# Shift and scale sums of a modulation: from TensorE during the expert gather to GpSimd and ScalarE ahead of it

## The reference, cut to what matters

```
mod_all = silu(c) @ ada_w + ada_b            # c: 1024, ada_w: 1024 x 6144
sh_m, sc_m, gt_m, sh_f, sc_f, gt_f = split(mod_all, 6)
h = rms_norm(x, norm_g[0]) * (1 + sc_m) + sh_m
x = x + gt_m * rms_norm(stick_breaking_mixer(h), norm_g[1])
h = rms_norm(x, norm_g[2]) * (1 + sc_f) + sh_f
x = x + gt_f * rms_norm(swiglu_ffn(h), norm_g[3])
```

## Time and profile before

| | |
|---|---|
| median of 3 runs | 2371.11 us (2367.22 to 2376.46) |
| the profiled execution's own time | 2365.49 us |
| its span | 2363.7 us |
| mean granted TensorE clock | 0.83 |
| PE, DVE, ACT, POOL busy | 76%, 55%, 37%, 38% of the span |
| moved by DMA | 687.78 MB, 536.90 MB of it by the gather's queue |

### The profile page before, as it was taken

The page is one execution under the profiler, slowest core; times in us unless marked ns, Lnnn a source line. Parts: engine busy times, 40 slices in busy tenths (PEclk is TensorE's granted clock), DMA queues, the critical chain, the costliest instruction groups (busy, mean ns, idle before and its releaser), DMA issues. The chain is left out here.

```text
span 2363.7 us, 25240 instructions
## 1 busy us (share of the span) xinstructions
PE 1796.4 (76%) x8848; PEld 1117.7 (47%) x8848; DVE 1291.7 (55%) x2801; ACT 868.9 (37%) x2355; POOL 904.2 (38%) x699
## 2 busy tenths in 40 slices
PE   8898899868777787564443468885377897999998
PEld 6775676445435255110000014331055676888786
DVE  4633668877787665656767676566403623333201
ACT  3122344333444343233643353333225734222212
POOL 1300334374663444344555544445400122444343
PEclk9999888777788889786555679986579998999999
DMA  6111999999999999999999999999953011122121
GB/s 246 54 63 49 403 410 392 418 377 411 411 401 418 418 418 417 417 404 406 419 420 420 419 405 419 418 397 419 420 178 110 1 72 71 72 107 107 72 107 54
DMA packets 108494, 687.78 MB, mean 291 GB/s; under 512 B 12240, under 2 KB 13264, under 8 KB 40144
## 3 DMA queue, kind: packets, MB, share of 16 engines
q0 software_dynamic: 73728, 536.90, 55.3%
q1 hardware_dynamic: 34640, 149.27, 16.9%
HBM read 681.40 MB, written 2.10 MB: 289 GB/s over the span
## 5 line engine op out<-in xcount | busy, mean ns | idle before, releaser
L747 PE MATMUL ps<-arena 128*32 128x512 f32 (+5 forms) x4376 | 872.7, 587 | 377.0 <-ACT arena L1452 337.3
L1696 POOL DMA_INDIRECT arena<-in_experts,arena_u x512 | 608.6, 1189 | 770.9 <-PE ps L747 678.2
L2001 DVE CUSTOM_DVE_ANT_0 arena<-arena 128x1024 f32<-128x1024 f32 x512 | 653.2, 1281 | 384.3 <-DMA arena<-in_experts,arena_u 367.5
L747 PEld LDWEIGHTS ps<-arena 128*128 128x128 f32 (+2 forms) x4376 | 443.2, 167 | 735.5 <-ACT arena L1452 496.6
L1448 ACT ACTIVATE sel<-sel 128x1 f32<-128x1 f32 x512 | 102.8, 201 | 705.4 <-DVE sel L2001 697.7
L1717 POOL TENSOR_TENSOR r_low<-middle,r_low 128x1024 fp32r<-128x1024 f32 x74 | 178.7, 2415 | 463.5 <-ACT r_low L1533 463.5
L747 PE MATMUL ps<-r_low 128*128 128x512 f32 x1248 | 286.4, 391 | 5.3 <-DVE r_low L2059 3.8
L747 PEld LDWEIGHTS ps<-r_low 128*128 128x128 f32 x1248 | 234.6, 189 | 56.8 <-DVE r_low L2059 4.4
L1452 ACT ACTIVATE arena<-arena,sel 128x32 f32<-128x32 f32 x512 | 164.5, 321 | 16.8 <-ACT sel L1448 0.2
L1533 ACT ACTIVATE r_low<-middle 128x1024 fp32r<-128x1024 f32 x74 | 78.3, 1058 | 208.1 <-PE ps L747 208.1
L747 PE MATMUL ps<-upper,arena 128*128 128x384 f32 (+5 forms) x640 | 144.9, 412 | 3.2 <-issue 3.0
(11 more groups left out here) (203 smaller groups left out, 1721.2 us busy)
## 6 DMA issues: line engine op xcount, KB each, us to landing
arena<-in_w_front SPq DMA_DIRECT2D x88, 512.0 KB, 3.5
middle<-in_w_late SPq DMA_DIRECT2D x18, 2048.0 KB, 8.2
arena<-in_w_qkv SPq DMA_DIRECT2D x48, 512.0 KB, 10.7
gtrow<-in_w_ada SPq DMA_DIRECT2D x32, 512.0 KB
arena<-in_experts,arena_u POOLq DMA_INDIRECT x512
arena<-in_w_ada SPq DMA_DIRECT2D x16, 512.0 KB, 10.0
x<-in_x SPq DMA_DIRECT2D x4, 512.0 KB, 8.7
arena<-in_sub_keys SPq DMA_DIRECT2D x2, 1024.0 KB, 10.4
```

Source lines behind the costliest of these rows:

```text
L747: return nc.tensor.matmul(out_, lhsT, rhs, start=start, stop=stop_, skip_group_check=skip)
L1696: nc.gpsimd.indirect_dma_start(ring[n % RING], None, a["experts"], bass.IndirectOffsetOnAxis(ap=idxq[:, i % 4, k:k + 1], axis=0),).then_in ...
L2001: nc.vector.tensor_tensor_reduce(r[:, 0:D], r[:, 0:D], xrep[k % 4], 1.0, 0.0, ALU.mult, ALU.add, dots[:, n % 8:n % 8 + 1]).then_inc(s["dot ...
```

## The change

The weights of shift and scale are laid out by output on the host: row m of `w_mod` holds for output m * 128 + p the 1024 weights on partition p. silu(c) is put as a row on all partitions (crow, 4 KB at 60 KB of the arena, doubled since the halving comes in the sum). 35 stages ahead of the gather are marked (MARKS: cv 3 to cv 11 are marks 0 to 8, mu 1 and mu 3 are 9 and 10, the levels 11 to 16, s2 and pm 17 to 20, wo 0 to wo 7 are 21 to 28, q 1 to q 6 are 29 to 34). At mark m SP loads row m into gtrow[m % 2], once ScalarE has summed row m - 2; at mark m + 1 GpSimd multiplies it by crow; at mark m + 2 ScalarE sums it with `accum_out`. In a stage the engine does its own part first, then the mark's; SP does the mark's part first. TensorE's `modulation`, its waits for "mod", and ScalarE's copies go.

```diff
+MARK_STAGES = [("cv", u) for u in range(3, QKV)] + [("mu", 1), ("mu", 3)] + [("u", (1, lv)) for lv in range(1, LEVELS)] \
+    + [("s2", 0), ("s2", 1), ("pm", 0), ("pm", 2)] + [("wo", k) for k in range(OUT_UNITS)] + [("q", j) for j in range(1, 7)]
+def marks():
+    out = {}
+    for n, (at, h, stage, arg) in enumerate(STAGES):
+        if at < 0 and (stage, arg) in MARK_STAGES:
+            out[n] = len(out)
+    return out
...
-        mpair = gtrow[:, :, :].rearrange("p s (k n) -> p s k n", k=2)
+        crow = region(60, D)
...
-            def pair(u):
-                if u >= 2:
-                    sp.wait_ge(s["mfree"], u - 1)
-                sp.dma_start(mpair[:, u % 2], a["w_ada"][u // 4, :, u % 4 * 2:u % 4 * 2 + 2, :]).then_inc(m_pair[u % 2], 16)
+            def mod_rows(m):
+                if m is None or m >= MODS:
+                    return
+                if m < 2:
+                    sp.wait_ge(s["cs"], 1)
+                else:
+                    sp.wait_ge(s["mod"], m - 1)
+                sp.dma_start(gtrow[:, m % 2, :], a["w_mod"][m]).then_inc(m_pair[m % 2], 16)
...
+            sp.dma_start(crow, a["c_row"][0:1, :].broadcast_to([P, D])).then_inc(s["rows"], 16)
...
-            done = 2
-            for at, h, stage, arg in STAGES:
-                done = mod_pairs(at, done)
+            for n_stage, (at, h, stage, arg) in enumerate(STAGES):
+                mod_rows(MARKS.get(n_stage))
                 if stage == "p":
                     front_unit(FRONT * h + arg)
...
-            def modulation(k):
-                n, kd = k // 4, k % 4 * 2
-                pe.wait_ge(s["cs"], 1)
-                pe.wait_ge(m_pair[k % 2], 16 * (k // 2 + 1))
-                if kd == 0:
-                    pe.wait_ge(s["idx"], n + 2)
-                for lane in range(2):
-                    for j in range(4):
-                        ins = mm(ps[:, 5, 64 + 4 * n + j:65 + 4 * n + j], mpair[:, k % 2, lane, j * P:(j + 1) * P],
-                                 ccol[:, kd + lane:kd + lane + 1], kd + lane + j == 0, kd + lane == KD - 1, True)
-                ins.then_inc(s["mfree"], 1)
...
                         nc.scalar.activation(ccol[:, :], vec("c"), ACT.Tanh, scale=0.5)
+                        sc.wait_ge(s["rows"], 16)
+                        nc.scalar.activation(gtrow[:, 0, :], crow, ACT.Tanh, scale=0.5)
...
+            def mod_sum(m):
+                if 0 <= m < MODS:
+                    sc.wait_ge(s["mprod"], m + 1)
+                    nc.scalar.activation(gtrow[:, m % 2, :], gtrow[:, m % 2, :], ACT.Copy, scale=0.5,
+                                         accum_out=flat(modc)[:, m:m + 1]).then_inc(s["mod"], 1)
...
                     front_stage(h, stage, arg)
+                    mod_sum(MARKS.get(n_stage, 0) - 2)
...
-                if n % TOPK == 12 and i < N_MODC:
-                    sc.wait_ge(s["mfree"], 4 * i + 4)
-                    nc.scalar.activation(flat(modc)[:, 4 * i:4 * i + 4], ps[:, 5, 64 + 4 * i:68 + 4 * i], ACT.Copy, scale=0.5).then_inc(s["mod"], 1)
...
+            def mod_product(m):
+                if 0 <= m < MODS:
+                    pl.wait_ge(m_pair[m % 2], 16 * (m // 2 + 1))
+                    tt(gtrow[:, m % 2, :], gtrow[:, m % 2, :], crow, ALU.mult).then_inc(s["mprod"], 1)
...
                     front_stage(h, stage, arg)
+                    mod_product(MARKS.get(n_stage, 0) - 1)
                     if stage == "sel" and arg == 0:
                         for n in range(RING):
                             load(n)
...
-                        stt(ccol[:, :], ccol[:, :], 1.0, vec("c"), ALU.add, ALU.mult).then_inc(s["cs"], 1)
+                        stt(ccol[:, :], ccol[:, :], 1.0, vec("c"), ALU.add, ALU.mult)
+                        stt(crow, gtrow[:, 0, :], 1.0, crow, ALU.add, ALU.mult).then_inc(s["cs"], 1)
```

More of the change, by code:

```diff
@@ L248 @@
 STAGES = paced(front_plan(0) + front_plan(1))
+MARK_STAGES = [("cv", u) for u in range(3, QKV)] + [("mu", 1), ("mu", 3)] + [("u", (1, lv)) for lv in range(1, LEVELS)] \
[6 more added lines that the diff above has]
+    return out
+MARKS = marks()
 LAG_ACT = {"tr0": 2, "cv": 1, "pz": 2, "tr1": 2, "q": 2, "sc": 2}
@@ L616, in gate_pair @@
                     sp.wait_ge(s["gfree"], u - 1)
[L617 to L624, removed]
+                sp.dma_start(gpair[u % 2], a["w_ada"][u // 4, :, u % 4 * 2:u % 4 * 2 + 2, :]).then_inc(g_pair[u % 2], 16)
             xt = a["x"].rearrange("(t p) d -> t p d", p=P)
@@ L642, in _ @@
                 unit(k)
-            pair(0)
-            pair(1)
             def front_unit(k):
@@ L988, in front_stage @@
                     if arg == 0:
+                        pe.wait_ge(s["cs"], 1)
                         pe.wait_ge(s["scs"], 2 * Q_UNITS)
@@ L1122, in qkv_unit @@
                 ins.then_inc(s["used"], 1)
-            mods = iter(range(MODS))
-            k = next(mods)
             for n in range(LOADS):
@@ L1140, in _ @@
                     rotate(t)
-                if k is not None and mod_load(k) == n:
-                    modulation(k)
-                    k = next(mods, None)
                 front.upto(n)
@@ L1968, in front_stage @@
                     ve.wait_ge(s["gfree"], 4 * m + 4)
-                    ve.wait_ge(s["rows"], 16 * (m + 1))
+                    ve.wait_ge(s["rows"], 16 * (m + 2))
                     own.step(stt(gacc[:, m, :], ps[:, m, :], 0.5, rows[:, 0, :], ALU.mult, ALU.add))
@@ L2005, in _ @@
                     if n == TOPK * PH + 2:
[L2006 removed]
+                        ve.wait_ge(s["mod"], MODS)
                         own.step(tt(flat(modc), flat(modc), vec("ada"), ALU.add))
@@ L2116, in laid_out @@
         "sub_keys": g["sub_keys"][0].reshape(2 * PH, NK, P).transpose(2, 0, 1),
-        "w_front": np.concatenate(front), "w_late": np.concatenate(late), "w_qkv": np.concatenate([columns(w_qkv[:, :2 * D]), w_values]), "w_ada": chunks(adaw),
+        "w_front": np.concatenate(front), "w_late": np.concatenate(late), "w_qkv": np.concatenate([columns(w_qkv[:, :2 * D]), w_values]), "w_ada": chunks(adaw[:, 4 * D:]),
+        "w_mod": adaw[:, :4 * D].T.reshape(MODS, P, D), "c_row": g["c_2"][0][None, :],
         "experts": np.concatenate([g["expert_down"][0], g["expert_up"][0]], axis=1),
```

11 lines of the change are left out of this document (2 added, 9 removed).

## The result

The kernel before took 2372.1 us (median of 20 runs, 2364.4 to 2379.0), the changed one 2389.7 us (20 runs, 2378.5 to 2396.4). The ratio is 1.008, with a 95% interval of 1.007 to 1.009. The forecast was 2374 and "no change"; the measured time lies at the upper end of the range.

A forecast was written before the change was run, and what follows sets the result against it. The prediction took DMA bytes to bound the gather and TensorE's waits the part ahead: +21 ahead, +15 at the gather's start, -32 in it make +4, 2369.5; with +5.6 for the median, 2374 was taken, range 2356 to 2390.

The forecast's parts named there:

- so in the gather, time is bytes: Gather, about 236 to 1710 us: DMA engines busy without a gap, so removing bytes saves time; gain taken as 32 us.
- My lower bound of 24: Gather's stretch with modulation: if only VectorE's 24.1 us wait for gathered rows shrinks, the gain is 24 us.
- VectorE is the bound of the gather: Slower rival, loads 8 to 120: above some 95% busy, VectorE limits the gain to 24 us; 2387 at most, chance 0.22.
- The prediction's own sign of being wrong: Among the signs of being wrong: the gather's stretch shrinks by less than 24 us with VectorE at 90%.
- TensorE's relief: Faster rival, gather: the 14 us lost in the stretch with modulation go too; gain 46 us, 2360 or less, chance 0.12.
- The front: Everything ahead of the gather: the added row work costs 21 us in all, 16 to 30.
- the norms of q and k: Ahead of the gather: a square root stands behind a row sum on ScalarE, so VectorE waits; +1 us.
- the output norm: Ahead of the gather: ScalarE's square root stands behind a row sum, so TensorE waits; +2.8 us.
- SBUF: Ahead of the gather: two-input VectorE operations on the path lose some 0.8 us beside GpSimd products; +1.5 us.
- SBUF lock: Slower rival, ahead of the gather: products wholly block eight VectorE path operations, 10 us instead of 1.5; 2383, chance 0.08.
- the clock's: Growth steps ahead of the gather: TensorE runs at half speed after its two longer stalls; +3.5 us together.
- The start of the gather: First loads: last rows delay the first reduction by 19 us; DMA engines idle from 262 to 276, +15 us (8 to 20).

The follow-up runs named there:

- run 1: Kernel before without 30 of its 32 modulation transfers, TensorE's passes kept: 0.9973, 2364.4 us.
- run 2: Kernel before without 30 of its 32 modulation transfers and without 30 of the 32 rounds of TensorE passes: 0.9905, 2348.2 us.
- run 12: Changed kernel, fused VectorE rows all ahead of the gather, and the gather's reductions 8 to 119 over 512 of 1024 columns: 0.9818, 2328.6 us.
- run 11: Changed kernel, each row one fused VectorE operation, 13 marks in the delta rule, then one per 5 loads: 0.9961, 2362.9 us.
- run 9: Changed kernel, each row one fused VectorE operation, all between the delta rule's first level and wo 5: 0.9932, 2352.7 us.
- run 10: Changed kernel, each row one fused VectorE operation, all in the gather, one per 3 loads: 1.0047, 2382.3 us.
- run 4: Changed kernel with the marks of q 1 to q 6 moved earlier, so all rows are summed before the first selection: 1.0017, 2377.0 us.
- Run 6: Changed kernel with the products of rows 6 to 9 and 22 to 25 over 8 of 1024 columns: 1.0042, 2379.5 us.
- run 8: Changed kernel with all 32 rows in the gather on GpSimd and ScalarE, one per 3 loads: 1.0100, 2394.1 us.
- run 7: Changed kernel with 13 marks in the delta rule, then one per 5 loads in the gather, on GpSimd and ScalarE: 1.0029, 2378.2 us.

## Why the prediction was wrong

**The step that failed is "so in the gather, time is bytes".** The DMA engines were full in the stretch with modulation, and I took that as the bound and set the gain at 32 us, near the 36 of the bytes. Measured were 19.5 us up to load 128 and 22.6 in all. The bytes alone are worth about 6 us (run 1), and nothing in the stretch: 15.7 MB went away there and its length stayed. What the gain needed was TensorE's passes out (another 16 us, run 2), and then VectorE's work ended it (run 12). That a share of 1.00 does not say who sets the time is shown by run 1; my reading, not shown by a run of its own, is that a ring of eight loads keeps the DMA engines busy as long as the chain of reduction, weight and sum is only a little slower than they are. My lower bound of 24, VectorE's whole wait for data, was nearer, and even it was not a lower bound.

**The rival "VectorE is the bound of the gather" was the right one, with the wrong condition.** I let it decide at 95% busy. Runs 11 and 12 show it deciding at 78% (296.85 / 379.1, run 9): 24.6 us more cost 16.1, and 49.0 less gave 27.7; run 10 agrees. Its gain, 24, was right within 1.4 us (22.6). That its time, 2387, came within 3 is in part luck: its front and start were too cheap by 3 to 4 us each, and the 5.6 us that it adds for the median made up for that, since the changed kernel's profiled execution lay at its own median. The average also hid lumps that stood in the trace of before, where VectorE was 97% busy in a window in which the DMA share fell to 0.66:

```profile
480.00:490.00 10.00, 5.56 (x26) 3.90 (x27) 9.73 (x25) 5.81 (x19) 9.22 (x6) 0.67 0.66 234
```

Of the 38 slices of 10 us from 251 to 631, VectorE is at least 90% busy in 13 and TensorE at least 95% in 11. So I take VectorE's idle time elsewhere to be no room for the lumps; that is argued from these slices, not shown by a run. The prediction's own sign of being wrong, a stretch shorter by less than 24 us with VectorE at 90%, had the same mistake in it: 19.5 came with VectorE at 79% (298.0 / 377.5).

**"TensorE's relief"** was right about the engine and wrong about the size: without its passes out there is next to no gain, but VectorE takes over after 16 to 19 us of it.

**The front** was forecast at 21 and came to 27.7, inside 16 to 30. By steps: first growth 4.2 for 4.2, second 5.5 for 4.9; the norms of q and k 6.3 for 1 and the port's share; the delta rule 0.4 for 0; pool and the way to wo 0 3.2 for 2; the output norm 6.5 for 2.8 and the port's share; the scores 1.6 for 1. The mis-sized term is **SBUF, 1.5 where 7.1 were measured**, for which the earlier trace rows already held the hint, 0.77 us lost beside a product half as long. The rival "SBUF lock" had the mechanism right and nearly the size (10). The steps without port and clock are 15.9 (4.2 + 4.9 + 1 + 2 + 2.8 + 1), the port 7.1; the 4.7 left are the clock's and what I can't place, against 3.5. Half clock shows behind the waits at 50 and 64 us, as forecast, but also behind those at 87, 95 and 173: 0.57, 0.62, 0.66, 0.54 and 0.57 were granted in windows of 4 to 7.5 us there. The first of them cost nothing, since TensorE then waited for GpSimd at 64.33 anyway. Not all of the others are new either: the kernel before had 0.51 at the norms of q and k.

**The start of the gather** was right: 18.9 us for 19 late, a hole of 12.6 for 15, repaired by run 4 for 12.7 to 15.

The sum by forecast was +21 + 15 - 32 = +4; by the ledger +27.7 + 18.9 - 22.6 = +24 (with the start's term as lateness, whose part hidden by transfers is then in the 22.6). Of the 20 us between them 7 are the front's; the other 13 are a gain that wasn't there. By the medians the change is +17.6 and 6.4 us of the +24 are missing; from which row of the ledger they would have to be taken, one profile of each kernel doesn't tell.

**Left open.** Why the first issue varies from 231.0 to 238.7 us between kernels that do the same ahead of it isn't explained but for the clock, below. Run 6 doesn't part the port from the shorter chain. What the passes are worth with the bytes still there was not run. What delays VectorE's turns between loads, in detail, was not followed.

## What to carry to other kernels

A full DMA share over a prefetch ring doesn't prove that bytes are the bound: leave the transfers out and look, and after that add work to each engine in turn. Leaving out one kind of work at a time isn't enough where two bounds lie close together, as passes and bytes did here. An engine at 78% can be the bound of a pipeline of in-order programs: work put on it there cost two thirds of its length (run 11), while the same work where that engine waits for another (here the delta rule) was free. In these traces a GpSimd product that reads two inputs from SBUF held up VectorE's operations of the same kind until it ended. So one operation on VectorE of 1.22 us was cheaper than a product of 2.36 on GpSimd and a sum of 1.25 on ScalarE: with all rows in the gather, 2382.3 us (run 10) against 2394.1 (run 8), and even VectorE itself was busy for less, 336.2 us of the stretch against 351.9.

## What the runs showed of the hardware that was not expected

GpSimd's product stretched not only VectorE's plain operations but also the gather's multiply-and-sum: 1533 ns on average with products beside it (run 8), 1300 in the changed kernel's stretch without, and in run 9 a fused row took 2.28 us beside a mask and 1.22 alone.

The granted clock ahead of the gather differs from execution to execution, for programs that are the same there. In the kernel before it was 0.87 in the first 40 us and load 0 came at 235.5 (runs 7 and 8: 0.87 and 235.3); in run 2 it was 1.00 and load 0 came at 231.0 (run 11: 1.00 and 231.3):

```profile
0.00:40.00 40.00, 28.90 (x147) 25.89 (x148) 15.95 (x44) 13.75 (x27) 1.40 (x6) 1.00 0.84 319
```

Run 1 had 1.00 there too, but 0.87 and 0.83 from 160 to 231, and issued at 238.7. So a shift of 4 us in one profile can be the clock's alone; the ledger above compares two executions that both had 0.87 in the first 40 us, but from 160 to 200 us the kernel before had 1.00 and the changed one 0.87.
